# Attention scores of a GLA branch: order of the score matmuls, and the width and place of their output tiles

## The reference, cut to what matters

```python
b = jnp.cumsum(ab.astype(jnp.float32), axis=-2)
q_t = qb * jnp.exp(b)
k_t = kb * jnp.exp(-b)
att = jnp.where(mask, jnp.einsum('bhtd,bhsd->bhts', q_t, k_t), 0.0)
o = jnp.einsum('bhts,bhsv->bhtv', att, vb) + jnp.einsum('bhtd,bhdv->bhtv', q_t, S)
```

## Time and profile before

| | |
|---|---|
| median of three runs | 992.32 us (990.43 to 992.75) |
| profiled execution, its own time | 992.51 us |
| its span, first to last instruction | 990.8 us |
| TensorE busy in the span | 984.6 us (99%) |
| VectorE, ScalarE, GpSimd busy | 530.6, 414.3, 107.7 us |
| mean granted TensorE clock | 0.998 |
| the chain of work that ended last | TensorE 99% |

### The profile page before, as it was taken

How to read it: one execution, slowest core, us unless ns; L and a number is a source line. 1 busy time by engine, 2 the same in 40 slices (tenths; PEclk the granted TensorE clock), 3 DMA queues, 4 the chain that set the end, 5 groups by cost and what they waited for, 6 DMA issues and landing times.

```text
span 990.8 us, 17402 instructions
## 1 busy us (share of the span) xinstructions
PE 984.6 (99%) x6684; PEld 971.5 (98%) x6684; DVE 530.6 (54%) x691; ACT 414.3 (42%) x514; POOL 107.7 (11%) x102
## 2 busy tenths in 40 slices
PE   9999999999999999999999999999999999999998
PEld 7999999999999999999999999999999999999998
DVE  6857634236674568644454444445445444596442
ACT  7445335433344334534344343444433333364331
POOL 0000001101115354000000000000001323100000
PEclk9999999999999999999999999999999999999999
DMA  9535423355745334544443544444447444435541
GB/s 324 207 107 173 150 101 129 128 185 184 233 165 169 119 123 134 161 158 149 148 148 132 164 148 148 148 148 148 148 150 268 148 152 146 146 125 192 176 167 40
DMA packets 52902, 155.80 MB, mean 157 GB/s; under 512 B 6208, under 2 KB 17280, under 8 KB 52864
## 3 DMA queue, kind: packets, MB, share of 16 engines
q1 hardware_dynamic: 39824, 140.52, 42.5%
q10 hardware_dynamic: 13040, 14.75, 4.4%
HBM read 147.65 MB, written 7.60 MB: 157 GB/s over the span
## 4 chain that ended last, share of the span: by engine, by line
PE 99%; DMA 0%; ACT 0%; DVE 0%; SPq 0%; issue 0%; DVEq 0%; ACTq 0%
PE bank L1112 29%; PE bank L1113 28%; PE bank L1114 28%; PE bank L1165 1%; PE bank L1168 1%; PE bank L1174 1%; PE bank L1409 1%; PE bank L1406 1%; PE bank L1412 1%; PE bank L1290 1%; PE bank L1281 1%; PE bank L1201 1%; PE bank L1138 0%; PE bank L1139 0%; PE bank L1140 0%; PE bank L1352 0%
## 5 line engine op out<-in xcount | busy, mean ns | idle before, releaser
L636 DVE TENSOR_TENSOR w_lo<-w_raw,w_hi 128x1024 fp32r<-128x1024 f32 x252 | 314.4, 1251 | 384.1 <-ACT w_hi L343 216.8
L1112 PE MATMUL bank<-x_hi,w_hi 128*128 128x320 f32 x1216 | 378.2, 311 | 0.0
L1113 PE MATMUL bank<-x_lo,w_hi 128*128 128x320 f32 x1216 | 375.9, 309 | 0.0
L1114 PE MATMUL bank<-x_hi,w_lo 128*128 128x320 f32 x1216 | 375.8, 309 | 0.0
L343 ACT ACTIVATE w_hi<-w_raw 128x1024 fp32r<-128x1024 f32 x148 | 155.8, 1058 | 263.3 <-PE bank L1114 251.0
L1112 PEld LDWEIGHTS bank<-x_hi,w_hi 128*128 128x128 f32 x1216 | 228.4, 188 | 0.8 <-issue 0.2
L1113 PEld LDWEIGHTS bank<-x_lo,w_hi 128*128 128x128 f32 x1216 | 228.4, 188 | 0.2
L1114 PEld LDWEIGHTS bank<-x_hi,w_lo 128*128 128x128 f32 x1216 | 228.4, 188 | 0.0
L540 ACT ACTIVATE w_hi<-w_raw 128x1024 fp32r<-128x1024 f32 x96 | 101.7, 1059 | 104.9 <-PE bank L1114 104.9
L1112 PE MATMUL bank<-m_hi,w_hi 128*128 128x320 f32 x448 | 138.4, 309 | 0.0
L1114 PE MATMUL bank<-m_hi,w_lo 128*128 128x320 f32 x448 | 138.4, 309 | 0.0
(11 more groups left out here) (232 smaller groups left out, 986.2 us busy)
## 6 DMA issues: line engine op xcount, KB each, us to landing
w_raw<-in_w_units SPq DMA_DIRECT2D x259, 512.0 KB, 3.3
state_dec<-in_s ACTq DMA_DIRECT2D x8, 512.0 KB, 5.9
out_st_dec<-state_dec ACTq DMA_DIRECT2D x8, 512.0 KB, 4.5
h<-in_x_t ACTq DMA_DIRECT2D x4, 640.0 KB, 6.3
out_y<-pe_out ACTq DMA_DIRECT2D x16, 160.0 KB, 2.1
x_sb<-in_x_t SPq DMA_DIRECT2D x7, 320.0 KB, 8.4
w_raw<-in_w_units SPq DMA_DIRECT2D x2, 256.0 KB, 4.2
out_st_prompt<-state ACTq DMA_DIRECT2D x1, 512.0 KB, 3.0
```

The lines of the kernel that those rows point to most:

```text
L636: dve.tensor_tensor(wlo[:, q], raw[:, q], whi[:, q].bitcast(F32), ALU.subtract).then_inc(lo_ready, 1)
L1112: pe.matmul(acc, h, hi[:, k0 + k, :], start=first and k == 0, stop=False)
L1113: pe.matmul(acc, h, lo[:, k0 + k, :], start=False, stop=False)
L1114: m = pe.matmul(acc, l, hi[:, k0 + k, :], start=False, stop=last and k == UK - 1)
```

## The change

The four kinds of score matmul are ordered by the width of their output: first all with 128 output rows (lines 1232 and 1245 of before), then all with 64, then all with 32. The 64-row ones alternate between partitions 0 to 63 and 64 to 127 of their bank. The 32-token level is no longer eight matmuls with 128 stationary columns but sixteen of 32 by 32, whose outputs go round the four groups of 32 partitions of bank 6. VectorE and ScalarE read the outputs where they now lie; the mask for the new tokens is repeated on partitions 64 to 127, since its two inputs start on the same partition.

```diff
@@ ScalarE, copies of the scores
                     for sub in range(2):
                         r0, r1 = 2 * BLK * sub, 2 * BLK * sub + BLK
-                        part = bank[6][:, :].rearrange("p (c h t) -> p c h t", c=2, h=HB)
+                        part = bank[6][:, 0:P].rearrange("p (h t) -> p h t", h=HB)
                         for c, dst in enumerate((att0, att1)):
-                            act.activation(dst[r0:r1, :, r1:r1 + BLK], part[r0:r1, c, :, BLK * sub:BLK * sub + BLK],
-                                           ACT.Copy).then_inc(att_copied, 1)
-                    part = bank[7][:, :].rearrange("p (c h t) -> p c h t", c=2, h=HB)
+                            act.activation(dst[r0:r1, :, r1:r1 + BLK], part[r0 + BLK * c:r1 + BLK * c], ACT.Copy)\
+                               .then_inc(att_copied, 1)
+                    part = bank[7][:, 0:2 * P].rearrange("p (h t) -> p h t", h=HB)
                     for c, dst in enumerate((att0, att1)):
-                        act.activation(dst[0:64, :, 64:P], part[0:64, c, :, :], ACT.Copy).then_inc(att_copied, 1)
+                        act.activation(dst[0:64, :, 64:P], part[64 * c:64 * c + 64], ACT.Copy).then_inc(att_copied, 1)
@@ VectorE, mask of the new tokens' scores
-                    mask = con[0:DEC, C_ATS:C_ATS + DEC].bitcast(I32)
                     for h in range(HB):
-                        last = dve.copy_predicated(att_s[:, h, :], mask, bank[3][0:DEC, DEC * h:DEC * h + DEC])
+                        r0 = DEC * (h % 2)
+                        last = dve.copy_predicated(att_s[:, h, :], con[r0:r0 + DEC, C_ATS:C_ATS + DEC].bitcast(I32),
+                                                   bank[3][r0:r0 + DEC, DEC * (h // 2):DEC * (h // 2) + DEC])
@@ TensorE, the scores
                     for h in range(HB):
-                        pe.matmul(bank[3][0:DEC, DEC * h:DEC * h + DEC], k_mid[:, h, SEQ:T], q_mid[:, h, SEQ:T],
-                                  start=True, stop=True)
-                    for c in range(2):
-                        for h in range(HB):
-                            c0 = 64 * (HB * c + h)
-                            odd = q_dec[:, h, P * c:P * c + P].rearrange("p (c t) -> p c t", t=BLK)[:, 1::2, :]
-                            pe.matmul(bank[6][:, c0:c0 + 64], k_dec[:, h, P * c:P * c + P], odd, start=True, stop=True)
-                            pe.matmul(bank[7][0:64, c0:c0 + 64], k_64[:, h, c, :], q_64[:, h, c, :],
+                        pe.matmul(bank[2][:, P * h:P * h + P], k_128[:, h, :], q_128[:, h, :], start=True, stop=True)
+                    for h in range(HB):
+                        for c in range(2):
+                            pe.matmul(bank[7][64 * c:64 * c + 64, 64 * h:64 * h + 64], k_64[:, h, c, :], q_64[:, h, c, :],
                                       start=True, stop=True)
                     for h in range(HB):
-                        m = pe.matmul(bank[2][:, P * h:P * h + P], k_128[:, h, :], q_128[:, h, :],
-                                      start=True, stop=True)
+                        r0 = DEC * (h % 2)
+                        pe.matmul(bank[3][r0:r0 + DEC, DEC * (h // 2):DEC * (h // 2) + DEC], k_mid[:, h, SEQ:T],
+                                  q_mid[:, h, SEQ:T], start=True, stop=True)
+                    for h in range(HB):
+                        for g in range(4):
+                            t0 = P * (g % 2) + 2 * BLK * (g // 2)
+                            m = pe.matmul(bank[6][BLK * g:BLK * g + BLK, BLK * h:BLK * h + BLK], k_dec[:, h, t0:t0 + BLK],
+                                          q_dec[:, h, t0 + BLK:t0 + 2 * BLK], start=True, stop=True)
                     m.then_inc(att_done, 1)
@@ constants
-    c[:DEC, C_ATS:C_ATS + DEC] = (s // DEC_L == t // DEC_L) & (t >= s)
+    c[:, C_ATS:C_ATS + DEC] = np.tile((s // DEC_L == t // DEC_L) & (t >= s), (P // DEC, 1))
```

## The result

The changed kernel takes 986.38 us (median of five runs, 986.01 to 986.75), against 992.32 for the kernel before (five runs, 990.43 to 993.65). The ratio is 0.9934, 95% interval 0.9922 to 0.9947: faster, by 5.9 us. The forecast was 987.2, a saving of 5.1, and its range 985.8 to 989.5. Before going on, note how the runs of before scatter over 3 us and those of after over 0.7; that turns out to be part of the story.

The account below looks back on a forecast made before the run. TensorE, 99% of the chain, was taken as the bound. Score-job terms 2.565 + 0.205 + 0.69 + 0.15 + 0.92 + 0.14 + 0.55 = 5.22 us against 10.44 save 5.2, giving 987.2 us, range 985.8 to 989.5.

Parts of the forecast that it names:

- The bound: Whole kernel: TensorE, busy 984.6 of 990.8 us, sets the end; time it saves comes off unless another engine falls behind.
- the half clock: Score job before, from 140.44 us into the next step: TensorE at 1.2 instead of 2.4 GHz, costing 1.6 us.
- The wide part: Start of the score job: 24 passes with 128 rows, 23 gaps, 2.565 us; then a change to 64 rows, 0.205.
- The 64-row part: Score job, 24 passes in two groups side by side: 12 rounds, 0.69 us, then 0.15 for the change to 32.
- The way into the stream: Behind the score job: next step's first product, 0.11 us dearer, and two ordinary gaps, 0.55 us in all.
- the fifth: Score job: 32 small 32-row passes replace 16 of L1241, at 0.029 us each, 0.92 us in all.
- lower end: Lowest price for the 32-row passes: eight rounds of four at 0.032 us, 0.26 us in all.
- The rate of instructions: Narrow score passes: instructions come no faster than one pass in 0.058 us; saving 4.5, total 988.0 us; chance 0.13.
- overlap: 64-row and 32-row score passes run side by side; the rival without this loses 1.6 to 3.6 us, 988.9; chance 0.10.
- a drain at each change of group: Narrow score matmuls: each change of group costs like a change of shape, 0.26 us a matmul, 994.3 us; chance 0.03.
- The cover: VectorE masks and ScalarE copies behind the scores: 0 to 0.1 us added each, 4.8 us to spare before TensorE needs masks.

Follow-up runs that it names:

- the sorted kernel: Kernel before with the same matmuls, shapes and places unchanged, only sorted by stationary width (128, then 64): median 988.6 us, ratio 0.9958.
- the eightfold run: Changed kernel with its 32-row matmuls issued eight times over, 256 passes instead of 32: 8.86 us from first score pass to the next step's fourth product.
- the two one-group runs: Changed kernel with all 64-row, or all 32-row, matmuls in one partition group: 5.25 and 5.29 us from first score pass to the next step's fourth product.
- the mixed-order kernel: Changed kernel's narrow matmuls in their groups, but 32-row and 64-row ones alternating and bank 2's 128-row ones last: median 989.06 us, ratio 0.9961.

## What the prediction had right, and the step that failed

**The bound.** TensorE alone set the end, and the saving came through: 5.89 us in the score job, 5.94 in the medians. No engine fell behind.

**The mechanism.** All three losses that it named are there: changes of shape, wide loads for narrow work, and the half clock. The runs separate them. At the full clock the stretch is 8.91 us before. Order alone brings 6.58 (2.33 less). Of the 2.03 us from there to 4.55, the second 64-row group gives 0.70, the four 32-row groups 0.74, and the remaining 0.59 are the narrow weights in place of wide ones, less one change of shape. The half clock gave another 1.53, where 1.6 was forecast. Together 2.33 + 2.03 + 1.53 = 5.89. The shares depend on the way taken: with the narrow tiles first it is 1.67 for them and 2.69 for the order. Why the clock falls is the part that is argued and not shown; a fall occurred once in the sorted kernel too.

**The prices, step by step.** The wide part: its last pass starts at 135.92, 2.57 us behind the first (2.565 summed), and the change behind it takes 0.20 (0.205). The 64-row part with the change behind it: 0.69 + 0.15 = 0.84 forecast, 0.85 measured. The way into the stream: 0.55 forecast, 137.90 - 137.36 = 0.54.

**The step that failed** is the fifth, the price of the 32-row part. The path and the overlap were right; the size was not. The forecast took 0.029 us a pass from a middle between two ends, 0.92 + 0.14 = 1.06 us to the stream; measured are 0.39. Its lower end, eight rounds of 0.032, was right: 0.26, with 0.13 for the change back where 0.14 was summed. The whole error of the job, 5.22 - 4.55 = 0.67, is this one term. I had read "no row shows a higher sustained rate" as a reason against one, though nothing in the trace showed instructions as the limit either: L1235's gap of 0.058 against 0.1115 for twice the columns is what the array gives by itself. The 0.029 was half of that gap and stood on no row. In its place the runs show 0.032 us for a round of four, 0.008 a pass, in the changed kernel, and not above 0.0085 over 226 passes in a row. Both operands of a pass had been halved against L1235's, so the gap halved, and four groups shared it; the lower end should have been taken.

The Trainium skill, page "TensorE: Matmul & The Clock Gate", section "Wait — 56ns, not 53.3ns?", gives about 25 ns from start to start as a floor and about 62 ns of sequencer time with hardware decode off. Passes that go round four groups came every 8 ns here, below both figures; in one group they came every 32 ns, which the floor allows. No run shows whether hardware decode was on, so the 62 ns may simply not have applied.

**The rivals.** The rate of instructions fell by the eightfold run, overlap was shown by the two one-group runs, a drain at each change of group would have shown at L1239 and L1248 and does not. In none of eleven runs of the changed kernel is the mean clock below 0.999, and both profiles show 1.00 in the score job.

**The cover.** VectorE and ScalarE were said to add 0.1 us each at most. They added 0.34 (L822) and 0.40 (L417, L421), since instructions that follow each other on different partitions start later. TensorE's transposes behind the masks (L1255) begin at 144.50, 4.4 us behind the last of them, so it cost nothing; as a price it was too low by a factor of three or four.

**The median of before.** The forecast started from one profiled run with a half-clock stretch. Against a run of before without one the saving is 990.7 - 986.4, some 4.3 us; against its slowest cluster 9. A median of a kernel whose runs lie in steps depends on which step it hits: in five comparisons it was 992.2 to 993.4, and against the highest of these the changed kernel's saving was 6.9. That 987.2 came within 0.8 of 986.38 owes something to the median and the profile of before lying on the same step.

## What to carry to other kernels

Sort TensorE's small jobs by the shape of their tiles: every change of shape takes 0.13 to 0.2 us from the last start of one shape to the first of the next, where a further pass would have taken 0.11 or less, and up to another tenth for a first weight load that nothing hides; and it costs that on an engine whose busy share reads 99%. Put narrow outputs in different partition groups in turn, where they run side by side, and price a small fp32 pass by the wider of its two operands, which set the gap in all rows here (0.11 us at 128, 0.058 at 64, 0.032 at 32), and not by the smallest gap seen. If a kernel's runs lie in steps, look for a sparse stretch of TensorE in which the clock falls. Making it dense took most of the scatter away here, together with the time. And when small reads on VectorE or ScalarE follow each other, keep them on the same partitions as long as possible.

## What the runs showed of the hardware

- Four fp32 passes of 32 by 32 in four partition groups start within a round of 0.032 us (32 passes), and within 0.034 over 226 passes; then TensorE once stood for 2.2 us that the profile puts to "issue".
- A pass of 128 stationary columns over 64 moving ones takes the 0.11 us of one over 128; a round of 32 stationary over 64 moving takes the 0.058 of 64 over 64.
- The clock can fall on a TensorE that is never idle. It fell from 2.4 to 1.2 GHz behind 4.4 us of alternating shapes in one profile and 6.2 in another, and stayed up through all 5.0 us of them in a third; in the narrow, denser alternation (135.40 to 138.94 in the mixed-order kernel) it stayed up as well.
- VectorE and ScalarE instructions that follow each other on other partitions start about 0.1 us later than on the same ones: L822 0.24 instead of 0.13 us apart, L417 0.29 instead of 0.17.
